# Hybrid recurrent trunk: the first mixer's sample path as its own strand, an explicit order of the late mixer steps, a normalization tile by tile, and the output projection begun in two pieces

## The reference, cut to what matters

```python
def _layer(x, c, st, prm):
    mods = (silu(c) @ ada_w + ada_b)                      # modulation, 9 x 1024 per sequence
    x = residual(x, 0, _swiglu(modulate(x, 0), ...), 0.5)
    proj = modulate(x, 1) @ w_in
    o_rw  = _rwkv7_mix(...)   # 6 heads x 64, first mixer
    o_gla = _gla_mix(...)     # 4 heads, 48 x 96
    o_ml  = _mlstm_mix(...)   # 4 heads x 64
    x = residual(x, 1, concatenate([o_rw, o_gla, o_ml]) @ w_out, 1.0)
    x = residual(x, 2, _swiglu(modulate(x, 2), ...), 0.5)
```

```python
    y = _standardize(y, RW_GN_EPS) * gn_g + gn_b          # per head of 64
    out = (y + sum(r * k * r_k) * v) * g
```

## Time and profile before

| | us |
|---|---|
| three runs | 1860.99, 1849.41, 1867.94 (median 1860.99) |
| the profiled execution, its own time | 1865.12 |
| its span, first to last instruction | 1863.3 |
| PE busy in the span | 1722.8 (92%) |
| DVE, ACT, POOL busy | 975.1, 674.8, 170.4 |
| mean granted TensorE clock | 0.906 of full |

### The profile page before, as it was taken

How to read it: one execution, slowest core, us unless ns; L and a number is a source line. 1 busy time by engine, 2 the same in 40 slices (tenths; PEclk the granted TensorE clock), 3 DMA queues, 4 the chain that set the end, 5 groups by cost and what they waited for, 6 DMA issues and landing times.

```text
span 1863.3 us, 33349 instructions
## 1 busy us (share of the span) xinstructions
PE 1722.8 (92%) x14324; PEld 1553.6 (83%) x14324; DVE 975.1 (52%) x1627; ACT 674.8 (36%) x945; POOL 170.4 (9%) x217
## 2 busy tenths in 40 slices
PE   5999999989899789999999999999879986899997
PEld 2899998987778568999989999988867764799997
DVE  2444446585633467555464445458564346655544
ACT  2223335463211435433353333355432123533333
POOL 1000012002001022000120000110020011300011
PEclk9999999999855589999999999999998557999999
DMA  8555664433232135444635555643323212344442
GB/s 329 174 202 211 195 215 138 153 102 114 93 121 68 48 120 214 148 148 153 220 120 203 186 189 172 214 144 113 113 70 122 68 49 80 110 158 153 151 147 74
DMA packets 92370, 270.24 MB, mean 145 GB/s; under 512 B 27168, under 2 KB 29504, under 8 KB 91968
## 3 DMA queue, kind: packets, MB, share of 16 engines
q1 hardware_dynamic: 87808, 265.50, 41.9%
q10 hardware_dynamic: 4416, 2.62, 0.5%
HBM read 261.83 MB, written 6.26 MB: 144 GB/s over the span
## 4 chain that ended last, share of the span: by engine, by line
PE 79%; DVE 13%; ACT 4%; DMA 2%; issue 2%; POOL 0%; SPq 0%; DVEq 0%; ACTq 0%; POOLq 0%
PE psV L1866 11%; PE psV L1868 11%; PE psV L1867 11%; PE psA L1866 9%; PE psA L1868 8%; PE psA L1867 8%; PE psC L1881 2%; PE psV L701 2%; DVE wlo L2151 2%; DMA raw<-weights_dram 2%; ACT whi L2027 1%; DVE PJ L1387 1%; PE psV L1891 1%; PE psY L1881 1%; PE psV L1472 1%
## 5 line engine op out<-in xcount | busy, mean ns | idle before, releaser
L2151 DVE TENSOR_TENSOR wlo<-raw,whi 128x1024 fp32r<-128x1024 f32 x340 | 420.0, 1239 | 441.4 <-ACT whi L2027 438.8
L2027 ACT ACTIVATE whi<-raw 128x1024 fp32r<-128x1024 f32 x340 | 358.0, 1055 | 332.9 <-PE psV L1868 324.5
L1866 PE MATMUL psA<-XH,whi 128*128 128x320 f32 x1200 | 383.2, 319 | 34.3 <-DVE XL L2203 23.6
L1867 PE MATMUL psA<-XL,whi 128*128 128x320 f32 x1200 | 374.9, 312 | 0.0
L1868 PE MATMUL psA<-XH,wlo 128*128 128x320 f32 x1200 | 374.5, 312 | 0.0
L1866 PEld LDWEIGHTS psA<-XH,whi 128*128 128x128 f32 x1200 | 229.1, 191 | 55.2 <-issue 34.4
L1866 PE MATMUL psV<-XH,whi 128*128 128x320 f32 x816 | 259.9, 319 | 14.7 <-DVE wlo L2151 7.2
L1867 PE MATMUL psV<-XL,whi 128*128 128x320 f32 x816 | 256.6, 314 | 0.0
L1868 PE MATMUL psV<-XH,wlo 128*128 128x320 f32 x816 | 256.3, 314 | 0.0
L1867 PEld LDWEIGHTS psA<-XL,whi 128*128 128x128 f32 x1200 | 229.5, 191 | 0.3
L1868 PEld LDWEIGHTS psA<-XH,wlo 128*128 128x128 f32 x1200 | 229.1, 191 | 0.0
(11 more groups left out here) (378 smaller groups left out, 1947.5 us busy)
## 6 DMA issues: line engine op xcount, KB each, us to landing
raw<-weights_dram SPq DMA_DIRECT2D x456, 512.0 KB, 3.3
raw_own<-weights_dram SPq DMA_DIRECT2D x24, 512.0 KB, 5.5
raw<-weights_dram SPq DMA_DIRECT2D x8, 256.0 KB, 3.7
ZS<-st_rw_dram SPq DMA_DIRECT2D x2, 768.0 KB, 4.4
S<-st_gla_dram ACTq DMA_DIRECT2D x2, 768.0 KB, 5.4
o_glas_dram<-S SPq DMA_DIRECT2D x2, 768.0 KB
o_rws_dram<-ZS SPq DMA_DIRECT2D x2, 768.0 KB
CON<-consts_dram SPq DMA_DIRECT2D x1, 1288.5 KB, 10.6
```

Of the source, the lines that this page charges most:

```text
L1866: mm(out, whi[:, n % SPL, k], hi[:, kt], start=first, stop=False)
L1867: mm(out, whi[:, n % SPL, k], lo[:, kt], start=False, stop=False)
L2027: activation(whi[:, n % SPL], buffer(DENSE[n]), ACT.Copy).then_inc(hi_done, 1)
L2151: tt(wlo[:, n % SPL], buffer(DENSE[n]), whi[:, n % SPL].bitcast(F32), ALU.subtract).then_inc(lo_done, 1)
```

## The change

1. **Samples as a strand.** `tau == 2` leaves `rw_pe` and becomes a generator of its own, `rs`, which works in psC, the modulation's bank. ACT copies the read-out columns of AR beside WT (`rw_wr`), so that one matmul with 16 columns takes the place of one into psA and one into psY: 48 instead of 96 per layer.
2. **Explicit order.** The step counts go. `LATE` names the steps after the inversion one by one. It holds no `ada` and no `fold`: the quarters are dealt over the inversion alone. In layer 1 two of the six groups move behind the norm after `out`.
3. **Third mixer's outputs** (L1472 before): the four passes over tokens are dealt so that neighbouring matmuls take different halves of rows and columns; both banks of a head pair are open together.
4. **Normalization tile by tile.** Gate times scale, and bias times gate, are formed early (six DVE operations after chunk 1); variances go to psA, Ln reads them there with its epsilon as bias, and each of the three tiles is handed on by itself.
5. **Out begun in two pieces.** `hi.0`, `hi.1`, `hi.2` and `lo.0` to `lo.2` make one chunk each; PE does 5 places of `out` after the means and 10 after the variances.
6. The table of Ln and Exp is loaded by name at three places (`preload_act_table_set`).

```diff
-RW_INVERSE, RW_CHUNKS, RW_SAMPLES, RW_END = 9 + 2 * (max(LEVELS) - 1), 10, 3, 3
-GL_STEPS, ML_STEPS = 11, 13
+LATE = ("rw ml gl rw ml gl ml rw gl ml rw gl ml gl rw ml gl rw ml gl ml rw gl ml su rs rw rs su mix hi.0 rw rs lo.0 rw "
+        "hi.1 rw hi.2 lo.1 early.0 rw lo.2 early.1 rw").split()
+EARLY_FIRST = 5
...
-    together += spread([(rw[0], 1)] * (RW_CHUNKS + RW_SAMPLES - 1), other)
-    out += spread([(step, 1) for step in together], ada_groups(in_tail) if in_tail else [])
-    out += [("mix", L), ("hi", L)] + rw * 3 + [("lo", L), ("early", L)] + rw
+    out += spread([(step, 1) for step in together], ada_groups(in_tail))
+    out += [(name.split(".")[0], L, *map(int, name.split(".")[1:])) for name in LATE]
...
-    steps, left = layer_plan(1, groups(1, 1, 0, 1, 2, 3), (groups(1, 1, 4, 5), [], []), groups(1, 2, 0, 1, 2, 3, 4, 5), left)
+    steps, left = layer_plan(1, groups(1, 1, 0, 1, 2, 3), (groups(1, 1, 4, 5), groups(1, 2, 4, 5), []), groups(1, 2, 0, 1, 2, 3), left)
...
-                        for h, s in PAIRED[:RW_H * DB]:
-                            ins = mm(bank[p, j * NS + 8 * s:j * NS + 8 * s + 8], ZS[p, j, s],
-                                     WT[tau][p, j, 8 * s:8 * s + 8], start=True, stop=True)
-                        for h, s in PAIRED[:RW_H * DB]:
-                            ins = mm(psY[p, j * P + 8 * s:j * P + 8 * s + 8], ZS[p, j, s],
-                                     AR[p, 1, j, t0 + 8 * s:t0 + 8 * s + 8],
...
+            def rs_pe(pe, bV, bA, rt):
+                pe.wait_ge(*at("rw_inverse", 1))
+                pe.wait_ge(*at("rw_state", 16))
+                pe.wait_ge(*at("rw_wr", 2))
+                for h, s in PAIRED[:RW_H * DB]:
+                    ins = mm(two(psC[:, 0:RW_W], p, j, s), ZS[p, j, s], two(whole(WT[2]), p, j, s),
+                             start=(s == 0 and j == 0), stop=False, skip_group_check=True)
+                ins.then_inc(sem("rw_g_full"), 1)
+                yield
...
-                pe.wait_ge(*at("rw_y", 3))
+                pe.wait_ge(*at("rw_y", 2))
+                pe.wait_ge(*at("rw_ys", 1))
...
-                act.wait_ge(*at("rw_yc", 1))
-                A.do(activation(N3[:], N2[:], ACT.Square), sem("rw_gsq"))
-                rsqrt(A, N4[:], sem("rw_gsd"))
+                for j in range(RP):
+                    act.wait_ge(*at("rw_yc", j + 1))
+                    A.do(activation(N3[:, j], N2[:, j], ACT.Square), sem("rw_gsq"))
+                yield
+                for j in range(RP):
+                    bank = fA.take()
+                    A.do(activation(N4[:, j], bank[:, 0:TOK], ACT.Ln, bias=EPS[:]), sem("bankA_free"))
+                A.settle()
+                for j in range(RP):
+                    A.do(activation(N4[:, j], N4[:, j], ACT.Exp, scale=-0.5), sem("rw_gsd"))
...
-                    for part in (slice(64, 128), slice(0, 64)):
-                        for half in range(2):
-                            for h in (2 * j, 2 * j + 1):
-                                for tau in range(3 - half):
+                    for turn in range(2):
+                        for tau in range(3):
+                            for bank, part in zip(banks, parts):
+                                for i, h in enumerate((2 * j, 2 * j + 1)):
+                                    half = (turn + i) % 2
```

More of the change, by code:

```diff
@@ L405, in hybrid_trunk @@
         crow = keep.take("crow", [P, 8, 1 + DB])
+        EPS = keep.take("EPS", [P, 1])
         w2_at = keep.at
@@ L751, in rw_pe @@
                 yield
-                for tau, t0, w in TAUS:
+                for tau, t0, w in TAUS[:2]:
                     pe.wait_ge(*freed[tau])
@@ new lines, in rw_pe @@
+                    for half in range(2):
+                        c, s = 2 * tau + half, slice(64 * half, 64 * half + 64)
+                        bank = bV.open()
+                        pe.wait_ge(*at("rw_z", c + 1))
+                        for h in EVEN_ODD(RW_H):
+                            j, p = hp(h)
+                            ins = mm(bank[s, h * HD:(h + 1) * HD], WT[tau][p, j, s], Z[p, c % 2, j], start=True, stop=True)
+                            if h == RW_H - 2:
+                                rt.after(ins)
+                        f = bV.close(ins)
+                        for h in range(RW_H):
+                            j, p = hp(h)
+                            ins = mm(psY[p, j * P + 64 * half:j * P + 64 * half + 64], Z[p, c % 2, j],
+                                     AR[p, 1, j, t0 + 64 * half:t0 + 64 * half + 64],
+                                     start=(half == 0 and j == 0), stop=False, skip_group_check=True)
+                        if half:
+                            rt.after(ins)
@@ L839, in rw_act, with rs_vec, two @@
+            def rs_vec(vec, V, fV):
+                yield
+                bank = fV.take()
+                V.do(nc.vector.tensor_tensor(U0[2][0:NS], bank[0:NS, 0:RW_W], U0[2][0:NS], ALU.add), sem("bankV_free"))
+                V.mark(sem("rw_u8"))
+                yield
+                yield
+            def two(t, p, j, s):
+                return t[p, j * P:(j + 1) * P].rearrange("p (x t) -> p x t", x=2)[:, :, DS * s:DS * (s + 1)]
             def rw_act(act, A, fA):
@@ L1081, in rw_vec @@
+                    yield
+                for j in range(RP):
+                    bank = fV.take()
+                    V.do(tt(N2[:, j], YT[:, j], bank[:, 0:TOK], ALU.subtract), sem("rw_yc"))
+                V.settle()
+                for j in range(RP):
+                    V.do(tt(YT[:, j], N2[:, j], gg(j), ALU.mult))
                 yield
                 yield
-                for j in range(RP):
-                    bank = fV.take()
-                    V.do(tt(N2[:, j], YT[:, j], bank[:, 0:TOK], ALU.subtract), sem("bankV_free"))
@@ L1107, in rw_vec @@
-                for j in range(RP):
-                    V.mark(sem("mixed"))
+                    vec.wait_ge(*at("rw_gsd", j + 1))
+                    V.do(tt(YT[:, j], YT[:, j], N4[:, j], ALU.mult))
+                    V.settle()
+                    V.do(tt(YT[:, j], YT[:, j], BON[:, j], ALU.add), sem("rw_m"))
+                    if j:
+                        low(j - 1)
+                low(RP - 1)
             def shift_pool(pool, G):
```

223 lines of the change are left out of this document (103 added, 120 removed).

## The result

The changed kernel takes 1794.8 us (median of four runs, 1784.0 to 1797.5) against 1860.7 for the kernel before in the same rounds: a ratio of 0.963, interval 0.959 to 0.967, so 66 us less. Three later measurements of the same kernel gave 0.959 (0.955 to 0.963), 0.963 (0.958 to 0.969) and 0.963 (0.959 to 0.967).

What follows compares the result with a forecast made beforehand. Late stretch bound by PE's queue near half clock, inversion by PE-DVE passing, tail by handoffs. Terms -22 - 15 + 9 + 3.5 - 9 - 9.5 - 2 = -45 took 1861 to 1816 us, range 1796 to 1849.

Steps and rivals of the forecast that it cites:

- The quarters: Inversion: takes the modulation quarters and folds from the late stretch, partly hidden in PE's idle; +9 us layer 0, +3.5 layer 1.
- the new wait: Inversion: PE waits for ACT's copy of psC before `Yb`, let go some 1.4 us later than before.
- The gap-filling in the norm of layer 1: Norm of layer 1: 8 quarters go into a gap of 6.05 us, 2 us less.
- samples and passes: Late stretch, per layer: merging two sample sets saves 3.1 us, alternating the third mixer's passes saves 1.4.
- 8 us of idle: Late stretch: PE idle that surfaces once the quarters no longer cover it, 8 us per layer, bounds 4 and 17.
- the late stretch at 101.6 us: Late stretch, both layers: comes to 101.6 us, 22 us less in layer 0 and 15 less in layer 1.
- the tail at 19 us: Tail, start to last split: 19 us where 28.2 and 28.8 stood, 9 and 9.5 less.
- Cover lost: Rival, chance 0.24: late stretch becomes a chain of handoffs, removed quarters give their time back; 25 us more, 1841.
- The clock stays away in the tail: Rival, chance 0.04: PE's clock does not return in the tail, out costs 30 us more per layer; 1876.
- The copy of psY stays late: Rival, chance 0.05: copy still behind a late `mix` on ACT, tail gives 5 us instead of 18.5; 1830.
- The clock holds in the inversion: Rival, chance 0.12: more work between levels keeps the inversion at 2.4 GHz in both layers, 7 us less; 1809.

Runs made afterwards that it cites:

- e1: Kernel before with only the modulation quarters dealt over the inversion alone and two layer 1 groups moved behind the norm after out: 1839.9 us, ratio 0.989.
- e6: Changed kernel with each 16-column matmul of the samples' set split into two of 8 columns: 1802.4 us, ratio 0.968.
- e4: Changed kernel with the third mixer's passes over tokens back in the old order: 1801.0 us, ratio 0.970.
- e9: Changed kernel without the two named table loads the change added in the second and third mixer: 1806.9 us, ratio 0.970.
- e13: Kernel before with only the two named table loads added: 1853.4 us, ratio 0.997.
- e2: Changed kernel with the quarters dealt again over the inversion and the late steps up to the first samples step: 1808.5 us, ratio 0.974.
- e5: Changed kernel with the late steps in the old order (first states' update six steps earlier, third mixer's last step right before mix): 1796.3 us, ratio 0.965.
- e10: Changed kernel with the late steps in the old order and without the two added table loads: 1807.2 us, ratio 0.971.
- e11: Changed kernel with each engine in the first mixer's normalization waiting for all three tiles of the engine before it: 1797.0 us, ratio 0.966.
- e3: Changed kernel with ACT's three whi splits all ahead of the first mixer's last steps, so before its copy of psY: 1796.6 us, ratio 0.968.
- e8: Changed kernel with mix and all three whi splits right ahead of ACT's copy of psY: 1798.0 us, ratio 0.966.
- e12: Changed kernel with all 15 early places of out after the variances, none after the means: 1792.6 us, ratio 0.963.

## Why the prediction was too small

**The quarters: the right numbers, in layer 0's inversion by luck.** The inversions are +7.9 and +3.4 where I had +9 and +3.5, with the new wait in its place. But in layer 0 quarters and folds take 25.1 us in place of 12.7, so 12.4 more, and I had 5.5 of that hidden in PE's idle time. On balance none was: idle went from 11.7 to 12.3 us. The wait of 3.29 us for DVE became 3.65 for ACT. A wait of 3.04, which the earlier trace rows did not show, fell to 0.67, but a second one for the copy of psC, 1.60 us at the inversion's end, came in, which I had not named. First before, then changed:

```profile
507.85 0.85 PE L730 MATMUL psA<-TK,AM 64*64 64x64 f32 x21 [3.04 <-DVE Tt L1058]
```

```profile
516.01 0.85 PE L734 MATMUL psA<-TK,AM 64*64 64x64 f32 x21 [0.67 <-DVE Tt L1090]
...
527.11 0.62 PE L1929 MATMUL psV<-FOLD,MR 128*128 128x18 f32 x4 [1.60 <-ACT MR L2127]
```

What made up for the cover that failed is the clock, 0.92 in place of 0.83: the rest of PE's work took 5.1 us less. In layer 1 idle fell by 2.6, about as forecast. The gap-filling in the norm of layer 1 gave nothing where I had 2: the quarters fill 3.6 us, and then PE waits 2.41 more for the same DVE chain.

```profile
1540.12 1.10 PE L1919 MATMUL psY<-raw,CT 128*32 128x256 f32 x16
1543.63 0.39 PE L1904 MATMUL psA<-XH,whi 128*128 128x320 f32 x1 [2.41 <-DVE XL L2243]
```

From the last split to this matmul it takes 45.6 us, and 45.8 before. e1 gives the quarters 21 us in all; my terms for them make 17.

**Right in size: samples and passes.** Merging the sets saves 4.8 us at half clock (e6), where I had 3.1 at the mixed clock of its row; the passes save 1.3 against 1.4. On the passes the rule that the Trainium skill states (TensorEngine Tiling (Array Packing), Gotcha 1: PSUM Pressure), that different row tiles cannot access one PSUM bank simultaneously, would by my reading have given nothing; e4 shows 92 and 76 ns a record. That is no test of the rule by itself, though, and neither was L1478: neighbours in the new order change the half of the columns together with the half of the rows, and e4 brings back a wait besides. Which of these pays is not shown.

**Right number, wrong reason: 8 us of idle.** It is 7.4. But e9 shows 11.6 for this order without the two table loads, and I had not priced these in the late stretch at all, only 2.56 us in each tail. That price was wrong too: e13's tails fall by 2.6 and 3.0, but by luck, one load and the clock. In the changed kernel the loads are worth 4.2 in the late stretch and 1.4 in the tail, per layer. I took the idle time from the rows of a stretch whose cover was about to go, and forgot to ask what ACT would then be late with.

**Wrong: the late stretch at 101.6 us.** It is 95.5 and 92.5 in the profile and 96.1 and 91.0 in the mean of four. Idle, samples and passes account for under 1 us of the difference; the instructions that stayed ran at a higher clock. The line of the sum that failed is "layer 1 does the same work in the same order, so it comes to 101.6 too". The work is the same, the clock is not: layer 1 enters the stretch at full speed and has it again in the middle. Part of this could be read beforehand. Layer 1's own row stood at 0.55, layer 0's at 0.53, and the folds of layer 1 are in this row:

```profile
1423.30:1539.60 116.30, 3.47 (x16) 3.56 (x16) 0.55 0.23 72
```

The same terms taken from its own row, 116.3 - 12.6 - 3.5 - 3.1 - 1.4 - 6.6 + 8, give 97.1 us and not 101.6, which is 4.5 of the 9.1 that layer 1 came out shorter. Two stretches of layer 1 in the changed kernel:

```profile
1391.45:1396.30 4.85, 4.72 (x81) 3.54 (x82) 3.58 (x16) 0.42 (x2) 0.00 (x0) 1.00 0.77 225
...
1446.00:1462.00 16.00, 13.24 (x184) 9.59 (x182) 9.03 (x14) 6.20 (x6) 0.00 (x0) 0.82 0.01 2
```

A mean clock of 0.58 over 92.5 us means that about 14.8 us of it were at full (length times twice the clock less one), in the four profiles 14.8, 21.2, 18.3 and 18.3, and 11.5, 13.1, 7.9 and 9.7 in layer 0; in e1 8.3 in both. Each such us does nearly the work of two: six products with 320 columns take 3.57 us at the one level and 1.88 at the other (before and e13, layer 1). I had carried layer 0's mixed 0.53 over both layers. What decides how much full clock a late stretch gets I could not settle: neither the quarters (e1, e2) nor the loads (e9) set it, and the same kernel varies by 6 us in it. The order may have a share. Reckoned so from the table, both layers together have 26 to 34 us at full clock in the changed kernel, 23 to 32 in the variants that keep its order or move one step (e6 alone has 18), and 17 to 19 in the five profiles with the old order (before, e1, e13, e5, e10). With one profile for each of them this is a hint and not shown.

**Wrong: the tail at 19 us.** It is 14.0 to 14.4 in every profile of the changed kernel. The wait of 8.38 fell to 0.58, as said. But I had priced PE's part at a mixed clock, 4 for 15 products, 3.6 for the variances, 7 to the last split; measured are 2.6, 2.1 and 5.5. The first two are shorter because the clock was back 5.3 us into the tail, which is 4.7 after the first of the means; of the second row here only the first 1.2 us are at half:

```profile
623.13:627.20 4.07, 3.49 (x7) 2.31 (x8) 3.33 (x5) 2.33 (x4) 3.47 (x3) 0.50 0.08 20
627.20:637.47 10.27, 10.11 (x58) 8.89 (x56) 8.90 (x16) 5.66 (x12) 1.55 (x2) 0.94 0.43 147
```

The last term failed in another way: PE's 30 products ended 4.4 us after the variances, and the end came with DVE's last split, after the 5.5 us that I had named for DVE and ACT and set aside for a longer PE. The three are 4.4 of the 4.8 us in layer 0, 2.9 of them by the clock. Taken apart by undoing, the tail's 14 us are: handing on tile by tile 2.2 (e11), order 2.3 (e5), loads 1.4 (e9), both together 0.9 more (e10), splits of whi behind the copy 1 to 2 (e3, e8), early products in two pieces nothing (e12). The remaining 5 to 7 were not undone. By argument only they are the DVE work made early (scale and bias of gate and bonus), `mix` earlier, and the clock, which in both tails of the profile before came back 8 to 9 us after the first of the means and in e13 after 4.2 and 4.3.

**The rivals.** Cover lost: no, idle is 7.4. The clock stays away in the tail: no, it is full from 5 us on. The copy of psY stays late: no, 0.58. The clock holds in the inversion: it did. The same products that took 11.8 us at 0.57 in the earlier trace rows ran so, with two quarters more among them and the wait of 1.60 us at the end:

```profile
515.97:527.11 11.14, 9.29 (x209) 7.29 (x209) 1.04 (x3) 4.88 (x11) 0.00 (x0) 1.00 0.26 84
```

But e13, with its quarters where they were, ran its inversion at 0.91 too. So the added quarters are not needed for it; whether its missing table loads did it, or the one execution of the kernel before that I had read was an odd one, is open.

**The range.** Over the 71.9 us of the two profiles, against my 45, the late stretches make 15 of the difference, the tails 10, the small pieces and the inversions 4, less 2 for the norm. Most of it is clock, in one direction. My bounds took idle from 4 to 12 and the sample set from 3.1 to 9.2, but never let the clock of the late stretch move.

## What to carry to other kernels

Where a stretch runs at a mixed clock, give the clock a bound of its own in the sum: price what stays once at either level for the part that could change, and look at both layers of the same program for how far apart equal work runs; take each layer's sum from its own row. A table load, a wait or a handoff that costs nothing under cover has to be priced again when the cover is moved; ask of each engine what it will be late with. When a wait is filled and comes back one piece later, the engine it names is the bound there, and reordering the waiting one gains nothing.

## What the runs showed of the hardware

- The granted clock differs between executions of one program: in four profiles of the changed kernel the late stretch took 93.4 us at 0.57 to 98.4 at 0.54 in layer 0, and 88.3 at 0.62 to 92.5 at 0.58 in layer 1, with the same 7.4 us of idle. Two profiles of one such stretch can differ by 4 to 5 us.
- In the tail the clock returned 3 to 6 us after the first of the products with 320 columns, in 37 of the 40 tails of all profiles, whether PE had waited 0.58 us before it or 7 to 9 (e13 4.2 and 4.3; e1, layer 1, 3.9). In the other three, each with a wait of 8.4 to 9.0, it took 8 to 9 us (both of before, layer 0 of e1).
- A 64-row matmul with 16 columns costs nearly the same as one with 8 (264 and 251 ns at half clock; 96 of them in a row take about 5 us).
- A table load counts only where its chain is last: of two loads in a tail one showed in the time, both in the kernel before (1.28 us of an 8.38 us wait) and in the changed one (0.98 to 2.24).
- The ACTIVATE after a table load started 0.01 us after its end in e9, so the drain of 1380 ns that the Trainium skill states (ScalarE: Activation LUTs, What ACT_TABLE_LOAD costs) is not seen in this kernel.
